# A transformer block on one core: three inverse roots move from VectorE to GpSimd, transposes and logits interleaved, smaller router instructions

## The chip, the cores and the metric

The kernel runs on one core of a Trainium2 chip. Time is device microseconds from launch to end; the profile also gives the span from the first to the last instruction. Lower is better.

## What is computed

One layer over 512 tokens of width 1024: adaptive layer norm, a gated mixing part, a residual, and then a mixture of 16 experts in 4 groups. The change sits between the residual and the experts:

```python
x = x + g_m[:, None, :] * jnp.einsum('bsd,de->bse', merged, w_out[l])
hf = modulate(rmsnorm(x, norm_ffn_g[l]), sh_f, sc_f)      # (x * rsqrt(mean(x*x) + EPS) * g) * (1 + sc_f) + sh_f
logits = jnp.dot(t.astype(jnp.float32), router_w.astype(jnp.float32))      # t = hf, 512 x 16
probs = jax.nn.softmax(logits, axis=-1)
# sel = probs + bias; the group with the best sum of two; its two best experts; their weights
x = x + g_f[:, None, :] * grouped_moe(hf, router_w, router_bias, w_exp_gate[l], w_exp_up[l], w_exp_down[l])
return rmsnorm(x, final_norm_g)
```

## The kernel before, in words

Every engine has a program of its own, written out by hand, and semaphores order them. Tokens go in four tiles of 128 rows (t = 0 to 3), the tokens on the partitions. Large products are split products: a float32 weight is turned into two float32r halves (`hi` by ScalarE, `lo` by VectorE, L703), and TensorE makes three matmuls of them (L1254 to L1256).

Before the change's place TensorE makes the output product, whose last quarter gives two half tiles (0 and 1) of each token tile in the order (0,0), (0,1), (1,0) and so on to (3,1). Then, for each token tile:

1. VectorE's `residual(t, half)` (L942, L945; called by `mixed`) multiplies the half tile in PSUM by the gate and adds x. 
2. ScalarE squares the tile with a running sum (L612), which gives one sum per row in a column of `stats`.
3. VectorE's `normed(t)` makes the inverse root of the mean in ten instructions on 128x1 operands (`inv_rms_1`, L738 to L748), and then `hf = x * root * gff` (L951), counted in `hf_scaled`.
4. The shift `shf` is added: by GpSimd for tiles 0 to 2 (L456), by VectorE for tile 3 (L975). It is counted in `hf_ready`; SyncE then stores the tile to DRAM.
5. TensorE transposes the tile (`turn_normed`, L1462, eight 128x128 pieces), ScalarE copies it out of PSUM (`turned`, L241), and TensorE multiplies it with the router (`logits`, L1451, eight float32 matmuls with 16 columns, each of them two records in the trace). ScalarE's `turned(t)` for t of 2 or 3 waits for `logits(t-2)`, since `hfT` has two buffers.

GpSimd also has two `lo` halves to make (L450) before it comes to its first shift. After all logits VectorE makes the softmax, the choice of group and experts, and the mask `r_m` (L1034); TensorE counts, with the strictly triangular matrix `before` and with `ones`, each token's place in its expert's list (L1476, L1478); VectorE builds `info` and `pos1`, and `select(j, e)` (L1064) makes the one-hot rows `sel` in four comparisons. TensorE's `index(j, e)` (L1487) turns them into token numbers, and GpSimd fetches those rows with an indirect DMA. Then the experts begin: tiles of 128 tokens of one expert, TensorE making gate, up and down products, while the weights of the next tile stream in and are split. `select` is called once per tile there, too.

The order of VectorE's and TensorE's work around the change is a written list:

```python
mixed(0, 0); mixed(0, 1); normed(0); mixed(1, 0)     # VectorE; then for t = 1 to 3:
mixed(t, 1); mixed(t + 1, 0); normed(t)              # (no mixed(4, 0))
turn_normed(0); turn_normed(1); logits(0); logits(1) # TensorE
turn_normed(2); logits(2); turn_normed(3); logits(3)
```

Of the kernel before, what the change touches and what calls it, by code (L numbers as in the profile page):

```python
# [5 lines left out]
F32 = mybir.dt.float32  # L6
# [7 lines left out]
P = 128  # L14
# [30 lines left out]
def tokens_moe_kernel(nc, A, out):  # L45
# [18 lines left out]
    with ctx:  # L64
        def sb(name, shape, dt=F32):
            return ctx.enter_context(nc.sbuf_tensor(name, shape, dt))

        def sem(name):
            return ctx.enter_context(nc.semaphore(name))
# [7 lines left out]
        ones = sb("ones", [P, P])  # L77
        before = sb("before", [P, P])
        iota1 = sb("iota1", [P, P])
# [121 lines left out]
        def small(n):  # L201
            at[0] += n
            return rt[:, at[0] - n:at[0]]

        te_view = lambda a: a.rearrange("p (t e) -> p t e", t=NT)
        r_d, r_p, r_sel, r_top = (small(NT * E) for _ in range(4))
        r_m_all = small((NT + 1) * E)
        r_m = r_m_all[:, 0:NT * E]
        r_d3, r_p3, r_sel3, r_m3 = map(te_view, (r_d, r_p, r_sel, r_m))
# [6 lines left out]
        r_extra = small(1)  # L216
        sub_ready = sem("sub_ready")

        def mix_hi(act, activation, i):
# [15 lines left out]
        def turned(act, activation, t):  # L235

            for half in range(2):
                act.wait_ge(hf_t, 2 * t + half + 1)
                if t >= 2:
                    act.wait_ge(logits_mm, t - 1)  # L240
                activation(hfT[:, t % 2, 4 * half:4 * half + 4, :].rearrange("p k m -> p (k m)"),  # L241
                           ps[:, 5 * (t % 2) + half, :], ACT.Copy).then_inc(hfT_ready, 1)
# [148 lines left out]
        def _(pool):  # L391
# [3 lines left out]
            g.memset(ones[:, :], 1.0)  # L395
            g.memset(before[:, :], 1.0)
            g.memset(base[:, :], 0.0)
# [6 lines left out]

            g.affine_select(out=before[:, :], in_=before[:, :], compare_op=ALU.is_gt, fill=0.0, base=0,
                            pattern=[[1, P]], channel_multiplier=-1)
# [45 lines left out]

            pool.wait_ge(row_ready, 4)
            for t in range(NT - 1):
                pool.wait_ge(hf_scaled, t + 1)
                g.tensor_tensor(hf[:, t, :], hf[:, t, :], shf, ALU.add).then_inc(hf_ready, 1)  # L456
            pool.wait_ge(hf_saved, 16 * NT)
# [29 lines left out]
        def _(act):  # L487
# [119 lines left out]
            for t in range(NT):  # L607
                if t == NT - 1:
                    turned(act, A_, 0)
                    turned(act, A_, 1)  # L610
                act.wait_ge(x2_half, 2 * t + 2)
                A_(hf[:, t, :], x_tiles[:, t, :], ACT.Square, accum_out=stats[:, 24 + t:25 + t]).then_inc(sq2, 1)  # L612
            for t in range(2, NT):
                turned(act, A_, t)
# [74 lines left out]
        def _(dve):  # L689
# [257 lines left out]
            def normed(t):  # L947

                dve.wait_ge(sq2, t + 1)
                inv_rms_1(24 + t)  # L950
                V.scalar_tensor_tensor(out=hf[:, t, :], in0=x_tiles[:, t, :], scalar=stats[:, 24 + t:25 + t],  # L951
                                       in1=gff, op0=ALU.mult, op1=ALU.mult).then_inc(hf_scaled, 1)

            lo_n(O0 + 3, 3)
# [9 lines left out]
            mixed(0, 0)  # L964
            mixed(0, 1)
            normed(0)
            mixed(1, 0)
            for t in range(1, NT):
                mixed(t, 1)
                if t < NT - 1:  # L970
                    mixed(t + 1, 0)
                normed(t)
            dve.wait_ge(hf_scaled, NT)
            dve.wait_ge(hf_ready, NT - 1)
            V.tensor_tensor(hf[:, NT - 1, :], hf[:, NT - 1, :], shf, ALU.add).then_inc(hf_ready, 1)  # L975

# [3 lines left out]
                                 ALU.add))  # L980
            step(V.memset(r_m_all[:, NT * E:], 0.0))

# [18 lines left out]
            def rank(values, n, result):  # L1001
# [31 lines left out]
            done()  # L1033
            V.tensor_tensor(r_m.rearrange("p (g e) -> p g e", e=EG), top_g,  # L1034
                            r_gr.unsqueeze(2).broadcast_to(ge3), ALU.mult).then_inc(mask_ready, 1)
            dve.wait_ge(mask_ready, 1)

# [22 lines left out]
            def select(j, e):  # L1060

                dve.wait_ge(idx_mm, j)
                for t in range(NT):
                    ins = V.tensor_scalar(sel[:, t, :], iota1[:, :], base[:, ds(j, 1)], pos1[:, t, ds(e, 1)],  # L1064
                                          ALU.add, ALU.is_equal)
                ins.then_inc(sel_ready, 1)

# [183 lines left out]
        def _(pe):  # L1251
# [216 lines left out]
            turn_normed(1)  # L1468
            logits(0)
            logits(1)  # L1470
            for t in range(2, NT):
                turn_normed(t)
                logits(t)

            pe.wait_ge(mask_ready, 1)
            nc.tensor.matmul(ps[:, 2, 0:(NT + 1) * E], before[:, :], r_m_all, start=True, stop=False)  # L1476
            for t in range(1, NT + 1):
                mm = nc.tensor.matmul(ps[:, 2, t * E:(NT + 1) * E], ones[:, :], r_m_all[:, 0:(NT + 1 - t) * E],  # L1478
                                      start=False, stop=(t == NT))
# [127 lines left out]
```

## Time and profile before

| | |
|---|---|
| Runs | 820.35, 821.66 and 824.33 us, median 821.66 |
| The profiled execution | 820.3 us, its span 817.7 us |
| Mean granted TensorE clock | 0.962 of full speed |
| Busy: TensorE, VectorE, ScalarE, GpSimd | 755.9, 609.1, 373.8, 196.4 us |
| Last dense product before the change's place ends | about 438.7 us from the span's start |
| First expert matmul | 476.37 us |

Times inside the kernel are microseconds from the start of the span. PE is TensorE, DVE is VectorE, ACT is ScalarE, POOL is GpSimd. "[idle before <-releaser]" at the end of a row says how long the engine had stood still before it and who ended that.

### The profile page before, as it was taken

The numbers are of one execution on the slowest core, as the hardware profiler recorded it, in microseconds if no ns is written. First come the engines' busy times: TensorE is split into PE (matmuls) and PEld (weight loads), VectorE is DVE, ScalarE is ACT, GpSimd is POOL, SyncE is SP. The second block draws the span as 40 slices with busy tenths as digits, with TensorE's granted clock in tenths as the row PEclk, the third lists the DMA queues.
The fourth block names the chain that finished last, engine by engine and source line by source line (L and its number), as shares of the span: only waits on it lengthen the run. The fifth ranks groups of instructions, "written<-read, shape, count | busy, mean of one in ns | idle before, by whom it ended". The sixth has DMA issues, their size and how long they took to land. (4 is left out here: it accounts for less than half of the span.)

```text
span 817.7 us, 10755 instructions
## 1 busy us (share of the span) xinstructions
PE 755.9 (92%) x3423; PEld 605.6 (74%) x3424; DVE 609.1 (74%) x806; ACT 373.8 (46%) x329; POOL 196.4 (24%) x74
## 2 busy tenths in 40 slices
PE   3879999999999999999999478999999999999982
PEld 1467888876787888887688467888888888888861
DVE  4972151785667565748558689999999999999976
ACT  3133352422413232323223357777777777777613
POOL 1000000500200000000043001544455555444552
PEclk9889999999999999999998579999999999999997
DMA  8979231422138192937362546599999999999652
GB/s 297 333 248 270 92 103 52 155 65 90 53 123 288 61 332 68 302 109 256 129 219 117 183 142 227 205 363 395 371 369 366 366 354 367 371 385 372 250 228 103
DMA packets 116339, 187.66 MB, mean 229 GB/s; under 512 B 6927, under 2 KB 66383, under 8 KB 115804
## 3 DMA queue, kind: packets, MB, share of 16 engines
q1 hardware_dynamic: 101660, 173.58, 60.4%
q0 software_dynamic: 4784, 7.95, 2.7%
q10 hardware_dynamic: 9872, 5.84, 2.4%
q8 instruction: 13, 0.21, 0.1%
q14 instruction: 10, 0.08, 0.0%
HBM read 180.47 MB, written 16.25 MB: 241 GB/s over the span
## 5 line engine op out<-in xcount | busy, mean ns | idle before, releaser
L703 DVE TENSOR_TENSOR wsplit<-raw,wsplit 128x2048 fp32r<-128x2048 f32 x132 | 299.5, 2291 | 89.9 <-ACT wsplit L494 64.3
L640 ACT ACTIVATE wsplit<-raw 128x2048 fp32r<-128x2048 f32 x96 | 184.0, 1920 | 74.1 <-PE ps L1256 74.1
L442 POOL DMA_INDIRECT expert_rows<-work,dest_now x15 | 108.2, 7212 | 114.3 <-DVE work L1160 114.3
L1254 PE MATMUL ps<-wsplit,hgT 128*128 128x512 f32 x272 | 110.0, 405 | 5.0 <-DVE hgT L1079 5.0
L1256 PE MATMUL ps<-wsplit,hgT 128*128 128x512 f32 x272 | 107.6, 396 | 0.0
L1255 PE MATMUL ps<-wsplit,hgT 128*128 128x512 f32 x272 | 106.6, 392 | 0.0
L1254 PE MATMUL ps<-hT,wsplit 128*128 128x512 f32 x256 | 102.4, 400 | 1.2 <-DVE mx L833 1.0
L1255 PE MATMUL ps<-hT,wsplit 128*128 128x512 f32 x256 | 101.0, 395 | 0.0
L1256 PE MATMUL ps<-hT,wsplit 128*128 128x512 f32 x256 | 101.0, 395 | 0.0
L755 DVE SCALAR_TENSOR_TENSOR raw<-raw,c_silu 128x256 f32 (+1 forms) x128 | 62.0, 484 | 17.7 <-DMA raw<-in_w_ada 13.7
L1254 PEld LDWEIGHTS ps<-wsplit,hgT 128*128 128x128 f32 x272 | 51.9, 191 | 15.5 <-DVE hgT L1079 5.6
L494 ACT ACTIVATE wsplit<-raw 128x2048 fp32r<-128x2048 f32 x20 | 38.2, 1915 | 49.5 <-PE ps L1256 20.7
L1256 PEld LDWEIGHTS ps<-wsplit,hgT 128*128 128x128 f32 x272 | 51.7, 190 | 12.2
L1255 PEld LDWEIGHTS ps<-wsplit,hgT 128*128 128x128 f32 x272 | 52.0, 191 | 11.0
L1254 PEld LDWEIGHTS ps<-hT,wsplit 128*128 128x128 f32 x256 | 48.0, 187 | 13.9 <-issue 1.9
L450 POOL TENSOR_TENSOR wsplit<-raw,wsplit 128x2048 fp32r<-128x2048 f32 x2 | 9.3, 4638 | 203.5 <-ACT wsplit L494 203.3
L1255 PEld LDWEIGHTS ps<-hT,wsplit 128*128 128x128 f32 x256 | 48.0, 187 | 12.2 <-issue 0.7
L1256 PEld LDWEIGHTS ps<-hT,wsplit 128*128 128x128 f32 x256 | 48.0, 187 | 11.9
L1254 PE MATMUL ps<-wsplit,aT 128*128 128x512 f32 x136 | 55.1, 405 | 1.5 <-DVE aT L1146 1.5
L1254 PE MATMUL ps<-wsplit,hT 128*128 128x512 f32 x128 | 52.1, 407 | 4.2 <-DVE hT L799 1.6
L584 ACT ACTIVATE wsplit<-raw 128x2048 fp32r<-128x2048 f32 x16 | 30.7, 1919 | 52.4 <-PE ps L1256 33.5
L1256 PE MATMUL ps<-wsplit,aT 128*128 128x512 f32 x136 | 53.4, 392 | 0.0
(240 smaller groups left out, 1224.5 us busy)
## 6 DMA issues: line engine op xcount, KB each, us to landing
raw<-in_w_exp_gate SPq DMA_DIRECT2D x32, 1024.0 KB
raw<-in_w_exp_up SPq DMA_DIRECT2D x32, 1024.0 KB
raw<-in_w_exp_down SPq DMA_DIRECT2D x32, 1024.0 KB
raw<-in_w_ada SPq DMA_DIRECT2D x24, 1024.0 KB
raw<-in_w_in SPq DMA_DIRECT2D x20, 1024.0 KB
expert_rows<-zeros ACTq DMA_DIRECT2D x4, 1024.0 KB, 9.1
raw<-in_w_branch_a SPq DMA_DIRECT2D x4, 1024.0 KB
raw<-in_w_branch_b SPq DMA_DIRECT2D x4, 1024.0 KB
```

Source lines behind the costliest of these rows:

```text
L442: g.indirect_dma_start(out=y_dram, out_offset=bass.IndirectOffsetOnAxis(ap=dest_now[:, 0:1], axis=0), in_=y, in_offset=None, bounds_check= ...
L450: g.tensor_tensor(wsplit[:, c + 2, 1, :], raw[:, c + 2, :], wsplit[:, c + 2, 0, :].bitcast(F32), ALU.subtract).then_inc(lo_ready, 1)
L494: A_(wsplit[:, n, 0, :], raw[:, slot, :], ACT.Copy).then_inc(hi_ready, 1)
L584: A_(wsplit[:, (j + 1) % 2, 0, :], raw[:, (j + 1) % 4, :], ACT.Copy).then_inc(hi_ready, 1)
L640: A_(wsplit[:, c, 0, :], raw[:, c, :], ACT.Copy).then_inc(hi_ready, 1)
L703: V.tensor_tensor(wsplit[:, n, 1, :], raw[:, slot, :], wsplit[:, n, 0, :].bitcast(F32), ALU.subtract).then_inc(lo_ready, 1)
L755: ins = V.scalar_tensor_tensor(out=acc, in0=raw[:, slot, k * CC:(k + 1) * CC], scalar=c_silu[:, k:k + 1], in1=acc, op0=ALU.mult, op1=ALU.add)
L1254: nc.tensor.matmul(out, w_hi, m_hi_, start=first, stop=False)
L1255: nc.tensor.matmul(out, w_hi, m_lo_, start=False, stop=False)
L1256: return nc.tensor.matmul(out, w_lo, m_hi_, start=False, stop=last)
```

## The change

Five edits. GpSimd makes the inverse roots of tiles 0 to 2, each of ten instructions, with a wait for the one before it after every instruction but the last; it still adds the shift to tiles 0 and 1, and VectorE adds it to tiles 2 and 3. VectorE's list is reordered so that more residuals stand ahead of each `normed`. TensorE's list becomes turn 0, turn 1, logits 0, turn 2, logits 1, turn 3, logits 2, logits 3, and ScalarE's copy of tile 1 stands behind its last square. The mask and the two constant matrices of the counting matmuls are float32r, and VectorE writes the mask twice, once for TensorE (`chosen`) and once for itself (`r_m`). The one-hot rows come from one subtraction on 128x4 and one comparison on 128x512.

```diff
+            def pool_step_done(ins):
+                pool_steps[0] += 1
+                ins.then_inc(pool_chain, 1)
+                pool.wait_ge(pool_chain, pool_steps[0])
+
+            def root(col):
+                m, z, q = stats[:, col:col + 1], nrm_pool[:, 0:1], nrm_pool[:, 1:2]
+                powers = [nrm_pool[:, 2 + j:3 + j] for j in range(3)]
+                for j in range(3):
+                    f = 4.0 ** (3 - j)
+                    pool_step_done(g.tensor_scalar(powers[j], m, f / D, f * EPS, ALU.mult, ALU.add))
+                pool_step_done(g.tensor_scalar(z.bitcast(I32), powers[2].bitcast(I32), -0.5,
+                                               float(0x5F3759DF - (2 << 23) - (1 << 31)), ALU.mult, ALU.add))
+                for j in range(3):
+                    pool_step_done(g.tensor_scalar(q, z, z, powers[j], ALU.mult, ALU.mult))
+                    ins = g.tensor_scalar(m if j == 2 else z, q, -3.0, z, ALU.add, ALU.mult)
+                    if j < 2:
+                        pool_step_done(ins)
+                ins.then_inc(pool_rms, 1)
             for t in range(NT - 1):
-                pool.wait_ge(hf_scaled, t + 1)
-                g.tensor_tensor(hf[:, t, :], hf[:, t, :], shf, ALU.add).then_inc(hf_ready, 1)
+                pool.wait_ge(sq2, t + 1)
+                root(24 + t)
+                if t < 2:
+                    pool.wait_ge(hf_scaled, t + 1)
+                    g.tensor_tensor(hf[:, t, :], hf[:, t, :], shf, ALU.add).then_inc(hf_ready, 1)
...
                 if t == NT - 1:
                     turned(act, A_, 0)
-                    turned(act, A_, 1)
...
-            for t in range(2, NT):
+            for t in range(1, NT):
                 turned(act, A_, t)
...
             def normed(t):
-                dve.wait_ge(sq2, t + 1)
-                inv_rms_1(24 + t)
+                if t < NT - 1:
+                    dve.wait_ge(pool_rms, t + 1)
+                else:
+                    dve.wait_ge(sq2, NT)
+                    inv_rms_1(24 + t)
...
             mixed(0, 0)
             mixed(0, 1)
+            mixed(1, 0)
             normed(0)
-            mixed(1, 0)
-            for t in range(1, NT):
-                mixed(t, 1)
-                if t < NT - 1:
-                    mixed(t + 1, 0)
-                normed(t)
-            V.tensor_tensor(hf[:, NT - 1, :], hf[:, NT - 1, :], shf, ALU.add).then_inc(hf_ready, 1)
+            mixed(1, 1)
+            mixed(2, 0)
+            normed(1)
+            mixed(2, 1)
+            mixed(3, 0)
+            mixed(3, 1)
+            normed(2)
+            shifted(2)
+            normed(3)
+            shifted(3)
...
-            V.tensor_tensor(r_m.rearrange("p (g e) -> p g e", e=EG), top_g,
+            V.tensor_tensor(chosen[:, 0:NT * E].rearrange("p (g e) -> p g e", e=EG), top_g,
                             r_gr.unsqueeze(2).broadcast_to(ge3), ALU.mult).then_inc(mask_ready, 1)
-            dve.wait_ge(mask_ready, 1)
+            step(V.tensor_tensor(r_m.rearrange("p (g e) -> p g e", e=EG), top_g,
+                                 r_gr.unsqueeze(2).broadcast_to(ge3), ALU.mult))
+            done()
...
-                for t in range(NT):
-                    ins = V.tensor_scalar(sel[:, t, :], iota1[:, :], base[:, ds(j, 1)], pos1[:, t, ds(e, 1)],
-                                          ALU.add, ALU.is_equal)
-                ins.then_inc(sel_ready, 1)
+                V.tensor_scalar(pos_e[:, :].unsqueeze(2), pos1[:, :, ds(e, 1)], base[:, ds(j, 1)], None,
+                                ALU.subtract).then_inc(pos_e_ready, 1)
+                dve.wait_ge(pos_e_ready, j + 1)
+                V.tensor_tensor(sel[:, :, :], iota1[:, :].unsqueeze(1).broadcast_to([P, NT, P]),
+                                pos_e[:, :].unsqueeze(2).broadcast_to([P, NT, P]),
+                                ALU.is_equal).then_inc(sel_ready, 1)
...
             logits(0)
+            turn_normed(2)
             logits(1)
-            for t in range(2, NT):
-                turn_normed(t)
-                logits(t)
+            turn_normed(3)
+            logits(2)
+            logits(3)
...
-            nc.tensor.matmul(ps[:, 2, 0:(NT + 1) * E], before[:, :], r_m_all, start=True, stop=False)
+            nc.tensor.matmul(ps[:, 2, 0:(NT + 1) * E], before[:, :], chosen[:, :], start=True, stop=False)
```

`shifted(t)` is the addition of L975 with its waits, for any t.

## Rows read from the trace of the kernel before

**Rows 1.** Busy time by stretch: PE, PEld, DVE, ACT, POOL, PE clock, DMA.
```profile
438.70:445.40 6.70, 6.19 (x56) 5.97 (x54) 5.06 (x20) 3.55 (x8) 2.39 (x2) 1.00 0.25 94
445.80:454.60 8.80, 8.79 (x40) 8.44 (x40) 3.15 (x8) 2.89 (x4) 0.00 (x0) 0.50 0.40 144
...
500.00:790.00 290.00, 288.51 (x1389) 240.20 (x1388) 280.58 (x282) 204.96 (x140) 146.30 (x33) 1.00 0.95 348
```

**Rows 2.** Timeline of PE: start, duration, line, idle time before.
```profile
438.53 1.91 PE L1462 MATMUL ps<-ident,raw 128*128 128x128 f32 x16
440.27 3.64 PE L1451 MATMUL ps<-router,work 128*128 128x16 f32 x32
444.43 1.09 PE L1462 MATMUL ps<-ident,raw 128*128 128x128 f32 x8 [0.51 <-POOL raw L456]
445.77 3.60 PE L1451 MATMUL ps<-router,work 128*128 128x16 f32 x16 [0.25 <-ACT work L241]
449.21 1.95 PE L1462 MATMUL ps<-ident,raw 128*128 128x128 f32 x8
450.99 3.60 PE L1451 MATMUL ps<-router,work 128*128 128x16 f32 x16
```

**Rows 3.** Timeline of DVE, the first and the last tile's norm.
```profile
425.39 1.39 DVE L745 SCALAR_TENSOR_TENSOR nrm<-nrm 128x1 f32<-128x1 f32 x1
...
427.91 1.28 DVE L951 SCALAR_TENSOR_TENSOR raw<-mx,stats,raw 128x1024 f32<-128x1024 f32 x1
429.11 0.69 DVE L942 TENSOR_TENSOR ps<-ps,tmp 128x512 f32<-128x512 f32 x1
...
430.44 0.69 DVE L942 TENSOR_TENSOR ps<-ps,tmp 128x512 f32<-128x512 f32 x1
...
444.49 0.28 DVE L738 TENSOR_SCALAR nrm<-stats 128x1 f32<-128x1 f32 x3 [1.22 <-ACT raw L612]
...
446.33 1.28 DVE L951 SCALAR_TENSOR_TENSOR raw<-mx,stats,raw 128x1024 f32<-128x1024 f32 x1
447.65 1.23 DVE L975 TENSOR_TENSOR raw<-raw 128x1024 f32<-128x1024 f32 x1
```

**Rows 4.** Timeline of POOL, the split halves and the first shift.
```profile
417.35 9.42 POOL L450 TENSOR_TENSOR wsplit<-raw,wsplit 128x2048 fp32r<-128x2048 f32 x2 [203.31 <-ACT wsplit L494]
429.34 2.41 POOL L456 TENSOR_TENSOR raw<-raw 128x1024 f32<-128x1024 f32 x1 [2.57 <-DVE raw L951]
```

**Rows 5.** Timeline of POOL in the first microseconds, its small instructions.
```profile
0.30 0.10 POOL L1597 MEMSET const-float32-0.0<- 128x1 f32 x1 [0.30 <-issue]
...
1.79 0.12 POOL L400 IOTA tok_i<- 128x4 int32 x1
2.07 0.29 POOL L402 TENSOR_SCALAR_AFFINE_SELECT ident<-ident 128x128 f32<-128x128 f32 x1 [0.16 <-POOL tok_i L400]
...
3.16 0.18 POOL L412 CAST tok_f<-tok_i 128x4 f32<-128x4 int32 x1
```

**Rows 6.** Timeline of ACT: two tiles copied out of PSUM, the last square.
```profile
439.16 2.07 ACT L241 ACTIVATE work<-ps 128x512 f32<-128x512 f32 x4 [0.41 <-PE ps L1462]
443.30 1.06 ACT L612 ACTIVATE raw<-mx 128x1024 f32<-128x1024 f32 x1 [2.07 <-DVE mx L945]
```

**Rows 7.** Timeline of DVE, the router's end and the first selection.
```profile
461.44 0.23 DVE L1038 TENSOR_TENSOR work<-work 128x64 f32<-128x64 f32 x1
461.58 0.22 DVE L1039 TENSOR_TENSOR work<-work,iota 128x64 f32<-128x64 f32 x1
...
463.81 0.23 DVE L1055 SCALAR_TENSOR_TENSOR pos<-ps,work 128x64 f32<-128x64 f32 x1 [0.30 <-PE ps L1478]
...
464.15 1.12 DVE L1064 TENSOR_SCALAR sel<-iota,base,pos 128x128 fp32r<-128x128 f32 x4
```

**Rows 8.** Timeline of PE, the counting matmuls and the first expert matmul.
```profile
461.97 1.81 PE L1478 MATMUL ps<-work,ones 128*128 128x64 f32 x8
...
476.37 0.79 PE L1254 MATMUL ps<-wsplit,hgT 128*128 128x512 f32 x1 [2.37 <-DVE hgT L1079]
```

More of the change, by code:

```diff
@@ L77, in tokens_moe_kernel @@
         ones = sb("ones", [P, P])
-        before = sb("before", [P, P])
+        before = sb("before", [P, P], F32R)
+        ones_r = sb("ones_r", [P, P], F32R)
+        chosen = sb("chosen", [P, (NT + 1) * E], F32R)
+        nrm_pool = sb("nrm_pool", [P, 5])
+        pos_e = sb("pos_e", [P, NT])
         iota1 = sb("iota1", [P, P])
@@ L206, in tokens_moe_kernel @@
         r_d, r_p, r_sel, r_top = (small(NT * E) for _ in range(4))
-        r_m_all = small((NT + 1) * E)
-        r_m = r_m_all[:, 0:NT * E]
+        r_m = small(NT * E)
         r_d3, r_p3, r_sel3, r_m3 = map(te_view, (r_d, r_p, r_sel, r_m))
@@ L217, in tokens_moe_kernel @@
         sub_ready = sem("sub_ready")
+        pool_chain, pool_rms, pos_e_ready = map(sem, ("pool_chain", "pool_rms", "pos_e_ready"))
         def mix_hi(act, activation, i):
@@ L395, in _ @@
             g.memset(ones[:, :], 1.0)
-            g.memset(before[:, :], 1.0)
+            g.memset(before[:, :].bitcast(F32), 1.0)
+            g.memset(ones_r[:, :].bitcast(F32), 1.0)
             g.memset(base[:, :], 0.0)
@@ L403, in _ @@
                             pattern=[[-1, P]], channel_multiplier=1).then_inc(consts, 1)
-            g.affine_select(out=before[:, :], in_=before[:, :], compare_op=ALU.is_gt, fill=0.0, base=0,
+            g.affine_select(out=before[:, :], in_=before[:, :].bitcast(F32), compare_op=ALU.is_gt, fill=0.0, base=0,
                             pattern=[[1, P]], channel_multiplier=-1)
@@ L453, in _ @@
             pool.wait_ge(row_ready, 4)
-            for t in range(NT - 1):
-                pool.wait_ge(hf_scaled, t + 1)
-                g.tensor_tensor(hf[:, t, :], hf[:, t, :], shf, ALU.add).then_inc(hf_ready, 1)
+            pool_steps = [0]
+            def pool_step_done(ins):
[16 more added lines that the diff above has]
+                ins.then_inc(pool_rms, 1)
+            for t in range(NT - 1):
+                pool.wait_ge(sq2, t + 1)
[3 more added lines that the diff above has]
+                    g.tensor_tensor(hf[:, t, :], hf[:, t, :], shf, ALU.add).then_inc(hf_ready, 1)
             pool.wait_ge(hf_saved, 16 * NT)
@@ L947, in normed, with shifted @@
             def normed(t):
-                dve.wait_ge(sq2, t + 1)
-                inv_rms_1(24 + t)
+                if t < NT - 1:
[3 more added lines that the diff above has]
+                    inv_rms_1(24 + t)
                 V.scalar_tensor_tensor(out=hf[:, t, :], in0=x_tiles[:, t, :], scalar=stats[:, 24 + t:25 + t],
                                        in1=gff, op0=ALU.mult, op1=ALU.mult).then_inc(hf_scaled, 1)
+            def shifted(t):
+                dve.wait_ge(hf_scaled, t + 1)
+                dve.wait_ge(hf_ready, t)
+                V.tensor_tensor(hf[:, t, :], hf[:, t, :], shf, ALU.add).then_inc(hf_ready, 1)
             lo_n(O0 + 3, 3)
@@ L965, in _ @@
             mixed(0, 1)
+            mixed(1, 0)
             normed(0)
-            mixed(1, 0)
-            for t in range(1, NT):
-                mixed(t, 1)
-                if t < NT - 1:
-                    mixed(t + 1, 0)
-                normed(t)
-            dve.wait_ge(hf_scaled, NT)
-            dve.wait_ge(hf_ready, NT - 1)
-            V.tensor_tensor(hf[:, NT - 1, :], hf[:, NT - 1, :], shf, ALU.add).then_inc(hf_ready, 1)
+            mixed(1, 1)
[8 more added lines that the diff above has]
+            shifted(3)
             dve.wait_ge(consts, 2)
@@ L980, in _ @@
                                  ALU.add))
-            step(V.memset(r_m_all[:, NT * E:], 0.0))
+            step(V.memset(chosen[:, NT * E:].bitcast(F32), 0.0))
             lg = ps[:, 4, 0:NT * E].rearrange("p (t e) -> p t e", t=NT)
@@ L1469, in _ @@
             logits(0)
+            turn_normed(2)
             logits(1)
-            for t in range(2, NT):
-                turn_normed(t)
-                logits(t)
+            turn_normed(3)
+            logits(2)
+            logits(3)
             pe.wait_ge(mask_ready, 1)
-            nc.tensor.matmul(ps[:, 2, 0:(NT + 1) * E], before[:, :], r_m_all, start=True, stop=False)
+            nc.tensor.matmul(ps[:, 2, 0:(NT + 1) * E], before[:, :], chosen[:, :], start=True, stop=False)
             for t in range(1, NT + 1):
-                mm = nc.tensor.matmul(ps[:, 2, t * E:(NT + 1) * E], ones[:, :], r_m_all[:, 0:(NT + 1 - t) * E],
+                mm = nc.tensor.matmul(ps[:, 2, t * E:(NT + 1) * E], ones_r[:, :], chosen[:, 0:(NT + 1 - t) * E],
                                       start=False, stop=(t == NT))
```

## The prediction

> **What bounds the kernel now.** I read the busy time by stretch first. From 500 to 790 us TensorE is busy 288.51 of 290 us at the full clock [rows 1]: the experts run at TensorE's pace, and what comes before them shifts the end one for one. A faster `select` there saves nothing, since VectorE (280.58 of 290) is not the one waited for. So the change is worth what it moves the first expert matmul, at 476.37 us [rows 8], which waits for a chain that begins at the last logits.
>
> Next the timelines of the four engines over that chain, to see who is late. TensorE leaves the dense product at about 438.7, does two transposed tiles and two tiles of logits at the full clock by 443.91, then waits 0.51 us for tile 2's shift and 0.25 us for ScalarE's copy, and from 445.77 it has no idle time: logits 2 to 449.37, turn 3, logits 3 to 454.59 [rows 2]. The reader is to see two prices for the same work: a tile of logits took 1.82 us (3.64 for 32 records), and then 3.60 us for 16; a turned tile 0.96 or 1.09 us, and then 1.95. The granted clock was 1.00 (2.4 GHz) up to 445.4 and 0.50 (1.2 GHz) from 445.8 to 454.6, although TensorE was busy 8.79 of those 8.80 us [rows 1]. So turns and logits do not bring the clock back here, however closely they stand.
>
> What set tile 3 before is VectorE. Its root of tile 3 starts at 444.49 and takes 1.84 us to the scale at 446.33, that 1.32 us to the shift at 447.65, which takes 1.23: `hf_ready` is 4 at 448.88 [rows 3]. TensorE's turn 3 began at 449.21 [rows 2], so there the two engines were level.
>
> **The roots on GpSimd.** Each is ten dependent instructions on 128x1. No such row exists. The nearest is the cast of 128x4, 0.18 us, and the one self-wait of that engine: the iota ends at 1.79 + 0.12 = 1.91, its follower starts at 2.07, 0.16 us later [rows 5]. 10 x (0.18 + 0.16) = 3.4 us a root, the value I take, being nearest in size and kind. Low bound: as quick as VectorE's 1.84 us [rows 3] (the 0.10 us memset [rows 5] would allow something near). High bound: each like the 0.29 us affine select, 10 x (0.29 + 0.16) = 4.5 us [rows 5].
>
> The place at which the first starts does not suffer: GpSimd ends its `lo` halves at 417.35 + 9.42 = 426.77 [rows 4], and VectorE's first root was itself held to 425.39 + 1.39 = 426.78 in a 128x1 instruction with two SBUF inputs [rows 3]. I read that as VectorE waiting for GpSimd. The GPSIMD Engine Reference of the Trainium skill, § Key points, names such a sharing of SBUF interfaces with VectorE instructions that have two SBUF inputs; the trace agrees, with this one row. By the page's § Engine selection, elementwise work with two inputs is about twice as slow on GpSimd; an estimate from that is 2 x 1.84 = 3.7 us a root, and the sum below would become +8.4 us. No run here shows which of the two it is.
>
> **The new chain.** In the order of the new lists; a residual costs 430.44 - 429.11 = 1.33 us, the scale 1.3 [rows 3], the square 1.2 from the residual's end to the root (1.06 of it [rows 6]), a handover to GpSimd 0.15 (429.19 to 429.34), a shift there 2.4 [rows 3, 4]; back from GpSimd I take 0.1.
>
> Root 0: 426.8 to 430.2. Scale 0 to 431.6 (VectorE stood still, its three residuals done at 426.4). GpSimd's shift 0 to 434.15; residual (1,1) and square 1 to 434.1. Root 1: 434.2 to 437.6. Scale 1 to 439.0, GpSimd's shift 1 to 441.55, residual (2,1) and square 2 to 441.5. Root 2: 441.6 to 445.0. Residuals (3,0), (3,1) are under it and end at 443.0. Scale 2 to 446.4, VectorE's shift 2 to 447.65: `hf_ready` 3, where the old order had 444.4 (turn 2 started at 444.43 [rows 2]). Then root 3 on VectorE 1.84, scale 1.3, shift 1.25: `hf_ready` 4 at 452.05 instead of 448.88. So all three roots lie openly on the chain, 3 x 3.4 us, while the VectorE time saved by it (3 x 1.84) is spent waiting. What was queued behind `normed`'s new wait is the next residual, and behind that the next square, which the next root needs; this is why the waits add.
>
> **TensorE's order.** Turns 0 and 1 and logits 0 are done by about 444.5 (turn 1 waits for shift 1 at 441.55, ScalarE's copy of it is 1.04 [rows 6] and stands behind the last square at 444.2). Then TensorE has nothing until 447.7, and what it does has become no denser than before; the clock is at 0.50. From there it is the bound: turn 2 1.95, logits 1 3.60, turn 3 1.95 (its tile was ready at 452.05), logits 2 3.60, logits 3 3.60: 447.7 + 14.7 = 462.4. Before, the last logits ended at 454.59: +7.8 us. Of it 3.2 are the later tile 2, and the rest is that logits 1, done at the full clock under other waits before, and logits 2, done before turn 3, now stand behind tiles that come later.
>
> ScalarE's copies and its table for Exp lie under the logits. SyncE's stores and the loads it holds until turn 3 move by 4.0 us (turn 3 ends at 455.2, before at 451.16), less than the router moves, so what they feed stays covered. GpSimd's later queue (clearing `hg`, the gathers) waits for the last logits as before. The extra memset in the first microseconds is under the first weight load.
>
> **Mask and counting.** VectorE writes the mask once more: 0.14 us, the spacing of 461.44 and 461.58 [rows 7]. The counting matmuls took 1.81 us for the eight records with 64 columns [rows 8]; as float32r they should be half the records or fewer, so VectorE's 0.30 us wait [rows 7] is gone, and no more than that can be gained. Bounds -0.16 and +0.14; I take -0.15.
>
> **Selection.** Now 1.12 us in four [rows 7]. New: one small instruction, 0.2 with its wait, and a comparison on 128x512; between the 0.22 us of 128x64 [rows 7] and the 1.23 of 128x1024 [rows 3] that is 0.22 + 448 x 1.05 ns = 0.69. Together 0.89: -0.2 us on the chain for `select(0, 0)`; bounds 0 and -0.4. The others are covered.
>
> **Sum.** +7.8 - 0.15 - 0.2 = +7.5 us. Against the profiled execution 820.3 + 7.5 = 827.8; against the median of the runs, 1.36 above it, 829.2. I say 828.5.
>
> **Rivals.**
> Small instructions on GpSimd are cheap: a root at VectorE's 1.84. Then each is 1.56 less, tile 2 is ready at 443.2 (it was 447.7 with the handover), tile 3 at 447.5; logits 1 falls partly before the clock does and ends about 446.9; turn 3 to 449.4, logits 2 to 453.0, logits 3 to 456.6: +2.0, less 0.35, +1.7 us: 822.7, no change that can be told. This is the case of the other side. It decides from a root of about 2.3 us down, where the sum falls below 4.1 us. For it speak the 0.10 us rows; against it the 0.16 us self-wait, paid nine times.
> The clock stays at 2.4 GHz: turn 3 452.05 to 453.0, logits 2 and 3 to 456.7, +1.7 us in all, again 822.7. Against it: the clock fell at 445.4 to 445.8 when TensorE had done more than it will now [rows 1, 2].
> Dear small instructions, 4.5 us a root: +3.3 more, +10.8, 831.8. Pointer scalars read by GpSimd speak for it.
> The delay is absorbed in the expert loop: TensorE idles only 1.5 us of 290 there [rows 1], so there is nothing to absorb it.
> Clock kept and cheap roots together would give logits 3 at 452.1, -2.8 us; nothing reaches 4 us of gain.
>
> **Chances.** Forecast 0.62 (range of its own 825.5 to 831), dear roots 0.16, cheap roots 0.13, clock kept 0.04, something that makes it faster 0.05. A measurement tells about 0.5%, 4.1 us, from no change. Slower by more than that: 0.78; within: 0.17; faster: 0.05. The range of 8 in 10 leaves out the outer half of the dear and most of the cheap case: 823.5 to 833.
>
> **What would show it.** GpSimd: thirty 128x1 rows, their spacing near 0.34 us, the three roots near 3.4 us each. VectorE: idle before each L951 of tiles 0 and 1 for about 4 and 3.5 us, of tile 2 for about 2. TensorE: turn 2 at about 447.7, the clock at 0.50 from before that, four logits with 3.60 us for the last three, the end at 462.4, the first expert matmul near 483.9, and a loop of unchanged length. Wrong it would be if spacing is under 0.23 us, if logits run at 1.82 us, or if tile 3 comes to TensorE before tile 2's logits could have started.

## The result, and the profile of the changed kernel

The changed kernel took 829.69 us (median of five, 828.89 to 831.56) against 821.66 (five runs by now, 820.35 to 824.33): a ratio of 1.0102, 95% interval 1.0084 to 1.012, or +8.4 us (6.9 to 9.9) on 821.66. Slower, as forecast, and 1.2 us from the time forecast. This closeness is in part luck: the edits that the forecast priced cost less than it said, and something that it left out made up for it. So the steps are read one by one. The profiled execution took 831.24 us, its span is 829.5.

Timeline of GpSimd in the changed kernel, the first root, its shift, the next root's start, and the end of the third:

```profile
416.71 9.36 POOL L455 TENSOR_TENSOR wsplit<-raw,wsplit 128x2048 fp32r<-128x2048 f32 x2 [201.70 <-ACT wsplit L526]
426.16 0.73 POOL L473 TENSOR_SCALAR nrm_pool<-stats 128x1 f32<-128x1 f32 x3
426.98 0.19 POOL L474 TENSOR_SCALAR nrm_pool<-nrm_pool 128x1 int32<-128x1 int32 x1
427.28 0.34 POOL L477 TENSOR_SCALAR nrm_pool<-nrm_pool 128x1 f32<-128x1 f32 x1
427.73 0.27 POOL L478 TENSOR_SCALAR nrm_pool<-nrm_pool 128x1 f32<-128x1 f32 x1
...
429.34 0.26 POOL L478 TENSOR_SCALAR stats<-nrm_pool 128x1 f32<-128x1 f32 x1
431.01 2.40 POOL L488 TENSOR_TENSOR raw<-raw 128x1024 f32<-128x1024 f32 x1 [1.41 <-DVE raw L985]
433.53 0.74 POOL L473 TENSOR_SCALAR nrm_pool<-stats 128x1 f32<-128x1 f32 x3
...
444.08 0.27 POOL L478 TENSOR_SCALAR stats<-nrm_pool 128x1 f32<-128x1 f32 x1
```

A root takes 3.44 us (426.16 to 429.60). Instructions with two per-partition scalars take 0.34, with one 0.27, with none 0.19, and the gap to the next is 0.10 to 0.11. The first root follows on the split halves within 0.09 us.

Timeline of VectorE in the changed kernel, the four scales, what they waited for, and the last shift:

```profile
429.63 1.29 DVE L985 SCALAR_TENSOR_TENSOR raw<-mx,stats,raw 128x1024 f32<-128x1024 f32 x1 [3.33 <-POOL stats L478]
...
437.01 1.28 DVE L985 SCALAR_TENSOR_TENSOR raw<-mx,stats,raw 128x1024 f32<-128x1024 f32 x1 [3.42 <-POOL stats L478]
...
444.38 1.28 DVE L985 SCALAR_TENSOR_TENSOR raw<-mx,stats,raw 128x1024 f32<-128x1024 f32 x1 [2.09 <-POOL stats L478]
445.70 1.23 DVE L992 TENSOR_TENSOR raw<-raw 128x1024 f32<-128x1024 f32 x1
...
448.68 1.28 DVE L985 SCALAR_TENSOR_TENSOR raw<-mx,stats,raw 128x1024 f32<-128x1024 f32 x1
450.00 1.23 DVE L992 TENSOR_TENSOR raw<-raw 128x1024 f32<-128x1024 f32 x1
```

VectorE waits 3.33, 3.42 and 2.09 us for the roots. Tile 2 is ready at 446.93, tile 3 at 451.23; the latter was 448.88 [rows 3].

Timeline of TensorE in the changed kernel; it answers to [rows 2] and [rows 8]:

```profile
438.69 1.04 PE L1508 MATMUL ps<-ident,raw 128*128 128x128 f32 x8
440.80 1.09 PE L1508 MATMUL ps<-ident,raw 128*128 128x128 f32 x8 [1.07 <-POOL raw L488]
441.72 2.07 PE L1497 MATMUL ps<-router,work 128*128 128x16 f32 x16
446.98 1.97 PE L1508 MATMUL ps<-ident,raw 128*128 128x128 f32 x8 [3.19 <-DVE raw L992]
448.74 3.43 PE L1497 MATMUL ps<-router,work 128*128 128x16 f32 x16
452.02 1.95 PE L1508 MATMUL ps<-ident,raw 128*128 128x128 f32 x8
453.76 6.85 PE L1497 MATMUL ps<-router,work 128*128 128x16 f32 x32
467.47 0.44 PE L1523 MATMUL ps<-chosen,before 128*128 128x80 f32 x1 [6.86 <-DVE chosen L1076]
467.70 1.00 PE L1525 MATMUL ps<-chosen,ones_r 128*128 128x64 f32 x4
...
481.84 0.79 PE L1300 MATMUL ps<-wsplit,hgT 128*128 128x512 f32 x1 [2.37 <-DVE hgT L1125]
```

TensorE waits 3.19 us for tile 2 and then never again until 460.61: it is the bound there, as forecast, with logits 1, 2 and 3 at 3.4 us each. Starts to read are 446.98, 448.74, 452.02, 453.76: a turn holds TensorE for 1.76 us, not the 1.95 of its row, since a row's end runs into the next one's start. The last logits end 6.0 us later than before (460.61 for 454.59), the first expert matmul starts 5.47 us later (476.37 in [rows 8]). The counting is five records instead of ten and VectorE no longer waits for it.

Busy time by stretch in the changed kernel (us; PE, PEld, DVE, ACT, POOL, PE clock, DMA share, GB/s):

```profile
444.00:446.00 2.00, 0.00 (x0) 0.00 (x0) 1.58 (x2) 0.45 (x1) 0.27 (x1) 0.50 0.03 12
448.74:460.60 11.86, 11.86 (x57) 11.75 (x56) 2.66 (x5) 3.08 (x4) 0.00 (x0) 0.50 0.53 191
481.84:487.60 5.76, 5.76 (x14) 4.50 (x15) 5.59 (x16) 3.56 (x3) 0.00 (x0) 0.50 0.43 106
560.00:740.00 180.00, 180.00 (x857) 147.87 (x856) 175.07 (x158) 129.72 (x88) 50.66 (x20) 1.00 0.99 364
```

and two of the same stretches of the kernel before:

```profile
476.40:480.00 3.60, 3.60 (x9) 2.86 (x10) 3.46 (x13) 3.54 (x3) 0.00 (x0) 0.56 0.51 150
...
560.00:740.00 180.00, 180.00 (x872) 150.22 (x871) 178.79 (x180) 132.11 (x90) 95.60 (x21) 1.00 1.01 371
```

Two things were not in the forecast. The first experts run 5.8 us at the half clock where it was about 3.2 (0.56 on average over 3.60 us), which costs half the difference, 1.3 us. And in the loop TensorE gets through 857 matmuls in 180 us instead of 872, at a clock of 1.00 in both and with no idle time in either. The index matmuls, one group a tile, show the period; first the kernel before, then the changed one:

```profile
560.77 0.50 PE L1487 MATMUL ps<-info,sel 128*128 x4
579.00 0.50 PE L1487 MATMUL ps<-info,sel 128*128 x4
```

```profile
568.75 0.50 PE L1534 MATMUL ps<-info,sel 128*128 x4
587.29 0.50 PE L1534 MATMUL ps<-info,sel 128*128 x4
```

18.23 us has become 18.54. Over 15 periods that is 4.7 us, more than half of the loss, and no edit touches TensorE's instructions there; only VectorE's selection, which feeds the index matmuls, was edited.

### The profile page after: what moved, and what is told of

It reads as the page before. It is cut to its first block, busy times and chain, and to the rows that moved or that the text cites. A ratio compares the mean times of both kernels' runs of the same rounds, so it can differ in the third digit from the quotient of the medians.

```text
span 829.5 us, 10664 instructions
## 1 busy us (share of the span) xinstructions
PE 763.8 (92%) x3418; PEld 609.4 (73%) x3419; DVE 602.1 (73%) x742; ACT 373.4 (45%) x329; POOL 138.2 (17%) x104
## 4 chain that ended last, share of the span: by engine, by line
PE 75%; DVE 11%; DMA 4%; ACT 3%; issue 2%; POOL 2%; ACTq 2%; SPq 1%; POOLq 0%; DVEq 0%
PE ps L1300 23%; PE ps L1302 23%; PE ps L1301 22%; PE ps L1544 2%; DVE wsplit L734 2%; ACTq L562 1%; ACT wsplit L526 1%; PE ps L1424 1%; PE ps L1497 1%; DMA mx<-in_x 1%; POOL wsplit L455 1%; DMA raw<-in_w_out 1%; DVE work L804 1%; PE ps L1578 1%; DMA raw<-in_w_in 1%
## 5 line engine op out<-in xcount | busy, mean ns | idle before, releaser
L1300 PE MATMUL ps<-wsplit,hgT 128*128 128x512 f32 x272 | 110.9, 408 | 5.0 <-DVE hgT L1125 5.0
L1301 PE MATMUL ps<-wsplit,hgT 128*128 128x512 f32 x272 | 109.1, 401 | 0.0
L1302 PE MATMUL ps<-wsplit,hgT 128*128 128x512 f32 x272 | 109.1, 401 | 0.0
L447 POOL DMA_INDIRECT expert_rows<-work,dest_now x15 | 44.4, 2961 | 121.1 <-DVE work L1206 121.1
L1301 PEld LDWEIGHTS ps<-wsplit,hgT 128*128 128x128 f32 x272 | 52.2, 192 | 11.8
L439 POOL DMA_INDIRECT work<-hf_rows,tok_idx x18 | 35.9, 1996 | 124.6 <-DVE row_dest L1120 90.4
```

The lines of the kernel that those rows point to most:

```text
L439: g.indirect_dma_start(out=hg, out_offset=None, in_=hf_dram, in_offset=bass.IndirectOffsetOnAxis(ap=tok_idx[:, 0:1], axis=0), bounds_check ...
L447: g.indirect_dma_start(out=y_dram, out_offset=bass.IndirectOffsetOnAxis(ap=dest_now[:, 0:1], axis=0), in_=y, in_offset=None, bounds_check= ...
L1300: nc.tensor.matmul(out, w_hi, m_hi_, start=first, stop=False)
L1301: nc.tensor.matmul(out, w_hi, m_lo_, start=False, stop=False)
L1302: return nc.tensor.matmul(out, w_lo, m_hi_, start=False, stop=last)
```

## The experiments

Ratios are to the kernel before on the same chip, with 95% intervals. The chips differ: the medians of the kernel before were 822.42 us beside runs 1 to 4, 821.71 beside 5 to 8, 821.81 beside 9 and 10, and 824.41 beside 11. So differences in us are differences of ratios, taken on 821.66, and not of the medians. An interval of one ratio is 1 to 2 us to either side. "From turn to expert" is the time from TensorE's first turn to the first expert matmul in the profile: 37.8 us before (438.53 to 476.37), 43.15 in the changed kernel. A profile is one execution, and where the first turn starts scatters: 438.53, 438.67, 441.23 and 438.99 us in the profiles of before and of runs 2, 8 and 6, where no edit touches the dense work ahead of it. The stretch behind it is compared for that reason.

**1. TensorE's and ScalarE's order undone in the changed kernel.**

```diff
-            turn_normed(2)
             logits(1)
-            turn_normed(3)
-            logits(2)
-            logits(3)
+            for t in range(2, NT):
+                turn_normed(t)
+                logits(t)
...
                     turned(act, A_, 0)
+                    turned(act, A_, 1)
```

> The changed kernel with TensorE's list and ScalarE's copies in the order of before (turn 0, 1, logits 0, 1, turn 2, logits 2, turn 3, logits 3). My theory, that the half of the loss is logits 1 and 2 standing behind later turns at the half clock: logits 1 is done in the gap before turn 2, the last logits end 2.5 to 3.3 us earlier than the changed kernel's (460.6 us, so 457.5 to 458), and the time is about 3 us below the changed kernel, still 3 to 6 us above before. Rival, that the late tile 3 alone sets the end (roots on GpSimd): no difference, since turn 3 cannot start earlier. Rival, that the expert loop's pace (18.54 us a tile in the changed kernel's profile, 18.23 before) belongs to the change: it stays at 18.54 here.

826.51 us, ratio 1.0050 (1.0027 to 1.0074): 4.3 us below the changed kernel. From turn to expert 40.7 us, 2.4 less than there, and the clock is back about 3.2 us after the first expert matmul instead of 5.8, which is worth another 1.3. Its period is 18.54 again, so the pace belongs neither to this order nor to the chance of one execution.

**2. That order alone, on the kernel before.**

> The kernel before with only TensorE's list and ScalarE's copies in the new order; roots all on VectorE. My theory: turn 2 at 444.4 as before, then logits 1 at or near the half clock, turn 3 at about 449, logits 2 and 3 behind it at 3.4 us each; the last logits end 3 us later than before's 454.6, time +3 us (+0.4%). Rival, that the order is harmless and only the roots cost: no difference. Rival on the loop: 18.23 us a tile if the pace of 18.54 comes with the roots or the selection.

825.02 us, ratio 1.0035 (1.0021 to 1.005), +2.9 us. TensorE's timeline:

```profile
444.44 1.09 PE L1461 MATMUL ps<-ident,raw 128*128 128x128 f32 x8 [2.16 <-POOL raw L456]
445.37 2.94 PE L1450 MATMUL ps<-router,work 128*128 128x16 f32 x16
448.95 1.97 PE L1461 MATMUL ps<-ident,raw 128*128 128x128 f32 x8 [0.64 <-DVE raw L974]
450.71 6.85 PE L1450 MATMUL ps<-router,work 128*128 128x16 f32 x32
```

From turn to expert it takes 40.65 us, 2.8 more than before. TensorE waits 2.16 us for tile 2, in which it used to do logits 1, and after tile 3 has come two tiles of logits are left instead of one, 6.85 us instead of 3.60. The period is 18.23.

**3. The GpSimd roots cut to one Newton step** in the changed kernel.

```diff
-                                               float(0x5F3759DF - (2 << 23) - (1 << 31)), ALU.mult, ALU.add))
-                for j in range(3):
+                                               float(0x5F3759DF - (1 << 31)), ALU.mult, ALU.add))
+                for j in (2,):
```

> The changed kernel with one Newton step instead of three in each GpSimd root (six instructions instead of ten; hf of tiles 0 to 2 is then off by up to 0.2%). My theory, that the three roots lie openly on the chain: each is 1.6 us shorter (3.44 to 1.84), tile 2 is ready 4.8 us earlier (turn 2 at about 442.3 instead of 446.98) and tile 3 likewise; the last logits end 3.5 to 5 us earlier, the time 4 to 5 us below the changed kernel. Rival, that the roots are covered by the residuals and TensorE's order alone costs: under 1 us of difference.

825.36 us, ratio 1.0041 (1.0021 to 1.006), 5.0 us below the changed kernel. TensorE's first turn and its last logits:

```profile
436.43 1.91 PE L1508 MATMUL ps<-ident,raw 128*128 128x128 f32 x16
...
446.62 6.85 PE L1497 MATMUL ps<-router,work 128*128 128x16 f32 x32
```

From the first turn, the last logits end after 17.0 us (436.43 to 453.47) instead of 21.9: 4.9 us for 3 x 1.6 = 4.8 us of roots taken away. The roots lie openly on the chain.

**4. The mask and the selection alone,** on the kernel before, their tensors declared where the change has them.

> The kernel before with only the float32r mask and the one-comparison selection. My theory: 0.4 to 0.6 us less between the last logits and the first expert matmul (21.78 before, 21.2 expected), nothing in the loop, since TensorE is the bound there: -0.5 us, not to be told from before. Rival: the comparison on 128x512 with two SBUF inputs slows the expert loop, 18.54 instead of 18.23 us a tile, and the time is 4 to 5 us above before.

827.11 us, ratio 1.0053 (1.0028 to 1.0078). My first theory fell: from the last logits to the first expert matmul it is 21.33 us, 0.45 less and as expected, but the period is 18.55 and the time 4.4 us above before. The rival's number was right; whether its reason was (the comparison with two SBUF inputs) took the next three runs.

**5. The tensors alone.** Nothing but unused tensors is added:

```diff
         before = sb("before", [P, P])
+        pads = [sb(f"pad{i}", [P, n]) for i, n in enumerate((P, (NT + 1) * E, 5, NT))]
```

> The kernel before with four unused tensors of the sizes of the change's new ones (128, 80, 5 and 4 words a partition) allocated at the change's place, so that everything from iota1 on, hT and hgT too, lies 896 bytes higher in SBUF; no instruction differs. Theory A, that TensorE's pace (0.2289 us a matmul of 512 columns in the loop of before, 0.2333 in the changed kernel) hangs on where the tensors lie: the loop's tile takes 18.54 us instead of 18.23, the time is 4 to 5 us above before. Theory B, that it hangs on the instructions (fewer counting matmuls, other selection): 18.23 us, no difference.

The period is 18.54 with the instructions of before, so the place of the tensors is the cause of the loop's pace. The time rises by less than I said, 823.47, ratio 1.0021 (1.0008 to 1.0034), +1.7 us, for in the first part of the kernel the same shift makes TensorE quicker. Rows of this run and, behind them, of before, for the second of the stretches (the first is above):

```profile
560.00:740.00 180.00, 180.00 (x859) 147.92 (x858) 175.69 (x175) 129.85 (x88) 94.43 (x20) 1.00 1.00 365
110.00:140.00 30.00, 30.00 (x133) 24.61 (x132) 11.02 (x17) 7.98 (x8) 0.00 (x0) 1.00 0.22 70
```

```profile
110.00:140.00 30.00, 30.00 (x130) 24.05 (x129) 10.63 (x14) 7.46 (x7) 0.00 (x0) 1.00 0.22 70
```

**6. The mask and the selection with their tensors behind all others:** the declarations of `ones_r`, `chosen` and `pos_e` stand after that of `work`, so that no old tensor moves.

> The float32r mask and the one-comparison selection on the kernel before, the new tensors allocated behind all others, so that no old tensor moves. Theory A (addresses): the loop's tile is back at 18.23 us, the time 0.5 us below before, and so 4 to 5 us below the same edits with the tensors in the middle. Theory B (instructions, above all the 128x512 comparison with two SBUF inputs): 18.54 us, time as in the run with the tensors in the middle, 4.7 us above before.

821.22 us, ratio 0.9992 (0.9977 to 1.0008), period 18.23. So the same instructions cost 5.0 us more or not by the place of three small tensors, and the wide comparison is harmless to the loop. The 0.5 us they should bring is in the interval but not shown.

**7. The whole change with its tensors behind all others.**

> The changed kernel with its four new tensors allocated behind all others. Theory A: first expert matmul at about 481.8 us as in the changed kernel, the loop at 18.23 us a tile, the time 5 us below the changed kernel, 3 to 5 us above before: what the roots and TensorE's order cost by themselves. Theory B: 18.54 us a tile and the time of the changed kernel.

826.55 us, ratio 1.0067 (1.0044 to 1.009), +5.5 us; first expert matmul at 482.01, period 18.25. This is what the roots, the orders and the small edits cost without the shift of the tensors. It is 2.9 us below the changed kernel, less than the 5 that I expected.

**8. The clock held up by extra matmuls,** on the kernel before.

```diff
+            def fill(n, bank=6):
+                for _ in range(n):
+                    nc.tensor.matmul(ps[:, bank, NT * E:], wsplit[:, 2, 0, 0:P], wsplit[:, 2, 0, 0:512 - NT * E],
+                                     start=True, stop=True)
```

with a wait, ahead of turn 0, until the split half that the extra matmuls read is there, and 2, 3, 3, 2, 4, 2 calls in bank 4 after turn 1, logits 0, logits 1, turn 2, logits 2 and turn 3, then 28 after logits 3, 4 after the counting, and 8, 16 and 9 around `index(1, 1)` and `turn(0)`.

> The kernel before with 81 extra matmuls of 448 columns on TensorE, whose results nobody reads, in its gaps between the dense product and the first expert matmul. Theory, that logits and turns cost double here only by the clock: it stays at 1.00 or comes back before the first expert, a tile of logits takes 1.8 us also for tiles 2 and 3, the first expert matmul comes 2 to 4 us earlier (472 to 474 us instead of 476.4), the first nine expert matmuls lose their half pace (1.6 us), and the time is 3 to 6 us below before. Rival, that the filling stands in the way of turns that are ready or that the clock falls all the same: no gain or a loss of 1 to 3 us.

818.18 us, ratio 0.9948 (0.9929 to 0.9967), -4.3 us. TensorE's timeline in it, and two of its stretches:

```profile
445.76 1.85 PE L1451 MATMUL ps<-router,work 128*128 128x16 f32 x16
447.46 0.86 PE L1458 MATMUL ps<-wsplit 128*128 128x448 f32 x3
448.16 1.03 PE L1470 MATMUL ps<-ident,raw 128*128 128x128 f32 x8
448.95 0.64 PE L1458 MATMUL ps<-wsplit 128*128 128x448 f32 x2
449.45 1.96 PE L1451 MATMUL ps<-router,work 128*128 128x16 f32 x16
...
453.42 1.96 PE L1451 MATMUL ps<-router,work 128*128 128x16 f32 x16
...
466.59 3.33 PE L1458 MATMUL ps<-wsplit 128*128 128x448 f32 x8
```

```profile
450.00:455.00 5.00, 5.00 (x41) 4.69 (x41) 1.53 (x5) 2.21 (x3) 0.00 (x0) 1.00 0.26 107
...
465.00:470.00 5.00, 4.28 (x14) 3.94 (x15) 3.68 (x20) 1.08 (x1) 1.09 (x1) 0.55 0.07 13
```

The logits of tiles 2 and 3 take 1.96 us instead of 3.60: their double price was the clock. From the first turn (441.23) the last logits end after 14.15 us, where it was 16.06. The clock fell later, at about 465, after a stretch (460 to 465) in which TensorE was busy 3.35 of 5.00 us, and eight extra matmuls then took 3.33 us and stood in front of the second index product; so from turn to expert it is 36.8 us, only 1.0 less, and my 2 to 4 us there were a miss. The first experts then ran at the full clock. This profile is of the highest of six runs (820.28). Three runs took 816.3 to 816.9 us with a mean granted clock of 0.978 to 0.980, the other three 819.5 to 820.3 with 0.973 to 0.976: where more of the clock is kept, more is gained.

**9. The place of the tensors by 64 and by 128 bytes,** on the kernel before: `pad = sb("pad", [P, 16])` or `[P, 32]` ahead of `iota1`.

> The kernel before with one unused tensor of 64 bytes a partition ahead of iota1, nothing else. So far a matmul of 512 columns took 0.2272 us where both operands lie in wsplit, 0.2289 or 0.2333 where one lies in hT, hgT or aT; which of the two changed with the place of hT (195392 bytes in, or 864 or 896 further). Theory: only the distance of the two operands' places modulo 256 bytes counts (wsplit is at 65664, 128 modulo 256; hT of before at 64). With 64 bytes more the distance is 0 as inside wsplit: 0.2272 us everywhere, the loop's tile 18.1 us instead of 18.23, the products with hT as moving operand 6 ns a matmul quicker (768 of them), 5 to 7 us below before in all. Rival, that 0.2272 belongs to operands of one tensor: 0.2289 and 0.2333 stay, no difference beyond 2 us. Rival, that another modulus counts: one of the levels changes in another way.

> The same with 128 bytes, so that hT is at 192 modulo 256, as in the changed kernel (896 bytes further). Theory (distance modulo 256 bytes): the changed kernel's levels, 0.2290 with hT as moving operand, 0.2333 in the loop, a tile of 18.54 us, 1 to 2 us above before. Rival, that a modulus of 128 or less counts, under which 128 bytes are no shift: the levels and the time of before.

With 64 bytes: 815.61 us, ratio 0.9916 (0.9891 to 0.994), -6.9 us, by one unused tensor. From turn to expert nothing changed (434.16 to 471.99, 37.8 us), the period is 18.14, and the two stretches read:

```profile
560.00:740.00 180.00, 180.00 (x876) 150.88 (x874) 179.74 (x176) 133.22 (x90) 96.86 (x20) 1.00 1.01 372
110.00:140.00 30.00, 30.00 (x135) 24.86 (x134) 10.69 (x15) 7.57 (x8) 0.00 (x0) 1.00 0.22 70
```

With 128 bytes: 825.13 us, ratio 1.0027 (1.0008 to 1.0045), +2.2 us, period 18.54, as with 896. Both came out as the distance modulo 256 says. By the table in the last section and the counts in the profile (768 matmuls with `hT` moving, 1608 with `hT`, `hgT` or `aT` stationary) the 64 bytes should bring 768 x 6.7 + 1608 x 1.3 ns = 7.2 us, an estimate as if each of them counted; measured 6.9.

**10. All that helped, together:** the edits of 6, the 64 bytes, and the filling with 2, 2, 1, 2, 5, 2 early calls, then 32, 9, 8, 16 and 9.

> The kernel before with the float32r mask and the one-comparison selection, their tensors behind all others, the 64 bytes of the run beside it, and extra matmuls of 448 columns in TensorE's gaps (2 after turn 1, 2 after logits 0, 1 after logits 1, 2 after turn 2, 5 after logits 2, 2 after turn 3, 32 after logits 3, 9 after the counting, then 8, 16 and 9 around the two index matmuls and the first gathered turn). Theory: the clock stays at 1.00 from the dense product to the first expert matmul; from the first turn to that matmul it takes 34 to 35.5 us (37.8 before, 36.8 with the first filling), and the three gains add: 0.5, 3 to 4 and what the 64 bytes give (5 to 7), so 9 to 12 us below before, 810 to 813 us. Rival: they overlap or the filling is late for its turns, 5 us or less.

808.34 us, ratio 0.9819 (0.9793 to 0.9844), -14.9 us, better than both kernels and than my 9 to 12. But the profiled execution took 815.9, the other five 806.44 to 809.6. In the profile the filling failed early:

```profile
440.00:445.00 5.00, 5.00 (x23) 4.78 (x23) 3.73 (x12) 2.12 (x4) 0.85 (x1) 0.50 0.26 105
445.00:450.00 5.00, 5.00 (x20) 4.68 (x21) 0.56 (x4) 0.00 (x0) 0.00 (x0) 0.50 0.26 105
...
455.00:460.00 5.00, 5.00 (x16) 4.48 (x16) 3.85 (x13) 2.17 (x2) 0.95 (x1) 0.50 0.99 344
...
465.00:470.00 5.00, 5.00 (x30) 4.64 (x29) 3.84 (x18) 0.00 (x0) 1.08 (x1) 1.00 0.00 2
```

so that the extra matmuls only stood in the way: 41.7 us from turn to expert (434.51 to 476.16) instead of 37.8. The other five runs can be judged by their mean granted clock: 0.979 to 0.984, where the profiled one has 0.969. A mean of 0.969 over 814 us is 50 us at the half clock, 0.982 is 29, an estimate from these two numbers; the difference, 21 us, is as long as the stretch from 440 to 460 that the profile shows at 0.50. So in those runs the clock was most likely kept there, though no profile shows it.

**11. The same with a denser early filling:** 3, 3, 3, 3, 5, 3.

> The combined kernel with more extra matmuls early on: 3 after turn 1, 3 after logits 0, 3 after logits 1, 3 after turn 2, 5 after logits 2, 3 after turn 3; the rest as it was. In the combined kernel's profiled execution (815.9 us; its other five runs 806.4 to 809.6) the clock was at 0.50 from logits 1 on, through the second turn and up to about 460 us, although TensorE had no idle time there. Theory, that the sparse filling holds the clock in most executions and not in that one: with the denser one the profiled execution shows 1.00 from the dense product to the first expert matmul, 36 us or less from the first turn to it, and all runs lie within 3 us of 808. Rival, that the clock falls in the same place and the other runs were no different in it: the profile shows 0.50 again and the median stays at 808 or rises by the 1 us of added matmuls.

810.88 us, ratio 0.9847 (0.9824 to 0.9869), 2.3 us above run 10 with intervals that overlap; the profiled execution 814.65, the others 809.71 to 813.16. The clock was 0.50 again from 440 to 450 us, and from turn to expert it took 41.15 us. The theory that a denser filling would hold it in every execution fell; the rival, that the other runs of run 10 had lost it too, is not borne out by their mean clocks, and here too the profiled run has 0.973 and the others 0.975 to 0.982. The first filling's profile, with the clock kept there, and these two, with it lost, differ in the places of the extra matmuls and of everything before them, and what decides is open. The traces were taken in the highest run of each of these three kernels.

## Why the prediction was right, step by step

**Bound and place:** right. TensorE is the bound in the loop (180.00 of 180), and the first expert matmul's delay went to the end undiminished: from that matmul to the end it is 342.2 us in run 7 and was 341.4.

**A root on GpSimd, 3.4 us:** 3.44 measured. The split of it was off (instructions of 0.19 to 0.34, gaps of 0.10 instead of 0.16), the sum not. The estimate from the Trainium skill, GPSIMD Engine Reference, § Engine selection, was 3.7, a little high; the measured 3.44 decides. It is no test of that factor, which the page gives for two inputs: GpSimd's instructions here read one tensor and scalars, and at one element a row fixed cost and waits are all there is. That all three lie on the chain: shown by run 3, 4.9 us for 4.8. The VectorE waits of "about 4 and 3.5, about 2" were 3.33, 3.42 and 2.09.

**Tile 2 and tile 3:** forecast 447.65 and 452.05, measured 446.93 and 451.23. Most of it is that GpSimd left its split halves 0.7 us earlier in this execution (426.07). That VectorE's first root of before had waited for these halves, which the forecast read from one row, holds in other traces: the instruction ends at 426.83, 424.28 and 423.27 us in runs 2, 5 and 10, GpSimd's halves at 426.81, 424.26 and 423.25.

**TensorE's order at the half clock, +7.8 us at the last logits:** right in kind, too large: +6.0. The term that was mis-sized is the 14.7 us from turn 2 to the end; it measured 13.6 (446.98 to 460.61), because I added durations of rows that overlap instead of distances between starts (449.21 to 450.99 in [rows 2] already said 1.78 for a turn). The other 0.7 is tile 2's. The order's own price is 4.3 us in the changed kernel by times and 3.7 in its trace (run 1), and 2.9 alone (run 2).

**Mask and selection, -0.35 us:** from the last logits to the first expert matmul 21.23 us instead of 21.78, -0.55 in these two traces. In the six traces with these edits and no filling it is 21.20 to 21.83 us, in the five without them 21.64 to 21.95; the means, 21.43 and 21.77, are 0.34 apart, about as forecast. Below what times can tell (run 6).

**The loop unchanged:** wrong, and the half-clock start of the experts was left out. The step that failed is one that the prediction never put as a term: that new tensors cost nothing by lying where they lie. It was worth +4.7 us in the loop, and about -2 in the first part: 768 matmuls with `hT` moving are 4.4 ns quicker each and 384 with `hT` stationary 4.4 ns slower, an estimate of -1.7, and run 5's first expert matmul starts 1.9 earlier, at 474.47, with 37.9 us from turn to expert as before. Runs 5 and 9 show the cause. The sum in the profiles: +5.5 up to the first expert matmul, +1.3 for the later return of the clock, +4.7 in the loop, together 11.5 of a span difference of 11.8. Between medians it is 8.4, since the first profile of before is among its lowest runs and that of the changed kernel among its highest.

By runs, in parts: the shift +1.7 (run 5), the small edits -0.5 (run 6), TensorE's order +4.3 (the changed kernel less run 1), and the roots +2.9, which is only what is left of 8.4 and so checks nothing. Each has an uncertainty of about 1 to 2.5 us. The check is run 7: all edits without the shift measured +5.5 (3.6 to 7.4), where these parts say 6.7, and the shift would then be worth 2.9. So the 7.5 of the forecast was about 2 us too much for what it named, with the clock's later return included, and the place of the tensors, which it did not know of, filled the gap by chance.

**The rivals:** cheap roots, dear roots (3.44 us, not 4.5), a kept clock and an absorbed delay are out by the rows above. What the "clock kept" rival priced is real, though: run 8 shows logits at 1.96 us once the clock is held.

## What to carry to other kernels

Moving a chain of tiny dependent instructions to an idle engine lengthens it, 1.84 to 3.44 us here, and if the engines then wait for each other in turn, every one of them lands on the chain; count the waits, not the busy time saved. When TensorE is at its half clock a reorder that puts work behind the last input costs about double what the same rows cost at full speed (3.43 us for a tile of logits here, and 1.82); sum starts, not durations. And when two kernels differ in a stretch that no edit touches, and no engine waits longer, compare TensorE's start-to-start times by operand pair: declare new tensors last, or try the hot ones at a few offsets of 64 bytes.

## What the runs showed of the hardware

The start-to-start time of TensorE's float32r matmuls of 512 columns, each with its weight load, at a granted clock of 1.00, depends on where its two operands lie. `wsplit` starts at 65664 bytes of a partition, 128 modulo 256. With one operand in `wsplit` and the other in `hT`, `hgT` or `aT` (all with one remainder), worked out from neighbouring starts in the timelines, several hundred in each cell:

| Kernel | Place of `hT` modulo 256 | 110 to 210 us: `hT` moving, `wsplit` stationary | Expert loop: `wsplit` moving, `hgT` or `aT` stationary |
|---|---|---|---|
| before | 64 | 0.2334 us | 0.2289 us |
| 64 bytes more | 128 | 0.2267 | 0.2276 |
| 128 bytes more | 192 | 0.2290 | 0.2332 |
| 864 bytes more (run 4) | 160 | 0.2333 | 0.2333 |
| 896 bytes more (run 5, and the changed kernel) | 192 | 0.2290 | 0.2333 |

With both operands in `wsplit` it was 0.2267 to 0.2277 in every kernel. All of this fits one number, the moving operand's remainder less the stationary one's: 0 is quickest, +64 is next, and +32, -32 and -64 are slowest. 128 and 896 bytes agree, which differ modulo 512, and 0 and 128 bytes do not, which are the same modulo 128. `wsplit` itself was never moved: that the difference counts and not each place by itself is read from the cells that agree with the roles exchanged. Other remainders weren't tried, nor other types or widths, and what in the chip does this is open. The whole is 3% of a matmul, and 0.8% of this kernel (run 9).

Second, the clock of 1.00 was held through a stretch of turns and narrow matmuls with extra wide matmuls between them (run 8, 440 to 465 us; before it fell at 445.4 to 445.8), but an arrangement that is not thinner lost it in its profile (run 11), with TensorE busy 5.00 of 5.00 us at 0.50. Third, GpSimd waits for itself in 0.10 us between 128x1 instructions here, where the one row of the profile of before said 0.16. Fourth, VectorE's 128x1 instruction with two SBUF inputs, 0.22 us otherwise, took 1.39 and ended with GpSimd's 128x2048 one that was under way (before; runs 2, 5 and 10 alike).
